# Loading every weight slot of a two-layer hybrid transformer step as two half-partition transfers

## What is computed

```python
mod  = silu(cond) @ w_ada[l] + b_ada[l]            # 1024 x 6144 per layer
proj = (rms_norm(x) * (1 + sc1) + sh1) @ w_in[l]   # 1024 x 1696
# three groups of heads read proj: latent attention (w_q_up, w_kv_up),
# a depthwise convolution, and a neighbourhood attention
x = x + g1 * (concat(heads) @ w_out[l])            # 1024 x 1024
h = rms_norm(x) * (1 + sc2) + sh2
# 16 experts, each token goes to 2 of them
hid = silu(h @ w_gate[e]) * (h @ w_up[e])          # 1024 x 512 each
x = x + g2 * sum_e gate[e] * (hid @ w_down[e])     # 512 x 1024
```

## Time and profile before

| what | us |
|---|---|
| median of 3 runs | 1395.42 (1394.6 to 1402.75) |
| the profiled execution, its own time | 1398.02 |
| its span in the trace | 1395.9 |
| PE busy | 1156.3 (83% of the span) |
| DVE busy | 850.8 (61%) |
| ACT busy | 662.0 (47%) |
| POOL busy | 215.2 (15%) |
| moved by DMA | 307.29 MB, of which 276.58 MB in SP's queue (q1) |

### The profile page before, as it was taken

The page is one execution under the profiler, slowest core; times in us unless marked ns, Lnnn a source line. Parts: engine busy times, 40 slices in busy tenths (PEclk is TensorE's granted clock), DMA queues, the critical chain, the costliest instruction groups (busy, mean ns, idle before and its releaser), DMA issues.

```text
span 1395.9 us, 15646 instructions
## 1 busy us (share of the span) xinstructions
PE 1156.3 (83%) x6086; PEld 947.8 (68%) x6086; DVE 850.8 (61%) x1039; ACT 662.0 (47%) x896; POOL 215.2 (15%) x187
## 2 busy tenths in 40 slices
PE   2999989998498999999829997889749899899980
PEld 1787666787477777777618776678737677777760
DVE  0147177513477888888641858832448788788853
ACT  1222444312276777787622133430237677677751
POOL 5002011000302211222003021100031122112200
PEclk9899989898699999999959996779769999999995
DMA  8865666311268899898733220002048898889833
GB/s 323 291 252 212 271 240 258 137 53 68 82 258 324 341 356 358 338 347 341 294 146 104 81 101 25 8 1 91 31 156 305 328 353 345 292 340 361 337 116 141
DMA packets 53179, 307.29 MB, mean 220 GB/s; under 512 B 11968, under 2 KB 12128, under 8 KB 19696
## 3 DMA queue, kind: packets, MB, share of 16 engines
q1 hardware_dynamic: 38304, 276.58, 52.3%
q0 software_dynamic: 13168, 23.39, 4.9%
q10 hardware_dynamic: 1632, 6.29, 1.2%
HBM read 305.00 MB, written 22.24 MB: 234 GB/s over the span
## 4 chain that ended last, share of the span: by engine, by line
PE 43%; DMA 23%; issue 15%; DVE 12%; POOL 4%; ACT 2%; POOLq 0%; DVEq 0%; ACTq 0%
DMA hg<-h_rows,h_at 19%; PE bank L926 19%; PE bank L669 9%; PE bank L658 3%; PE bank L918 3%; DVE conv_acc L1652 3%; POOL y_rows L619 2%; PE bank L786 2%; DMA ring<-wring_dram 1%; PE bank L680 1%; PE bank L713 1%; ACT y L1233 1%; PE bank L890 1%; DMA vecs<-vec_dram 1%; PE bank L772 1%
## 5 line engine op out<-in xcount | busy, mean ns | idle before, releaser
L1788 DVE TENSOR_TENSOR w_lo<-ring,w_hi 128x2048 fp32r<-128x2048 f32 x192 | 438.6, 2292 | 98.7 <-ACT w_hi L1203 98.3
L1203 ACT CAST w_hi<-ring 128x2048 fp32r<-128x2048 f32 x192 | 367.0, 1917 | 36.7 <-PE bank L926 36.7
L926 PE MATMUL bank<-w_hi,hgT_hi 128*128 128x512 f32 x512 | 203.8, 398 | 5.1 <-issue 3.2
L926 PE MATMUL bank<-w_lo,hgT_hi 128*128 128x512 f32 x512 | 201.2, 393 | 0.0
L926 PE MATMUL bank<-w_hi,hgT_lo 128*128 128x512 f32 x512 | 201.1, 393 | 0.0
L669 PE MATMUL bank<-ring,hT 128*128 128x256 f32 (+1 forms) x672 | 139.6, 368 | 2.1 <-DVE hT L1332 2.1
L669 PEld LDWEIGHTS bank<-ring,hT 128*128 128x128 f32 x672 | 122.0, 190 | 18.3 <-DVE hT L1332 2.6
L526 POOL TENSOR_TENSOR rstd<-ms,half 128x3 f32<-128x3 f32 (+3 forms) x14 | 39.8, 2842 | 516.2 <-DVE ms L1314 516.2
L619 POOL DMA_INDIRECT y_rows<-y,y_at x32 | 36.7, 1147 | 531.1 <-ACT y L1233 493.3
L926 PE MATMUL bank<-w_hi,hidT_hi 128*128 128x512 f32 x256 | 107.0, 418 | 9.9 <-DVE hidT_lo L1810 9.9
L926 PEld LDWEIGHTS bank<-w_hi,hgT_hi 128*128 128x128 f32 x512 | 97.1, 190 | 26.6 <-issue 7.0
(11 more groups left out here) (224 smaller groups left out, 1565.1 us busy)
## 6 DMA issues: line engine op xcount, KB each, us to landing
ring<-wring_dram SPq DMA_DIRECT2D x260, 1024.0 KB, 7.0
parts<-y_rows ACTq DMA_DIRECT2D x6, 1024.0 KB, 7.1
ring<-wring_dram SPq DMA_DIRECT2D x6, 640.0 KB, 4.3
h_rows<-h_tok POOLq DMA_DIRECT2D x2, 1536.0 KB, 5.9
bias<-na_bias_dram POOLq DMA_DIRECT2D x32, 64.0 KB, 5.5
x<-x_in_dram POOLq DMA_DIRECT2D x1, 1536.0 KB, 11.3
y_sample_dram<-x POOLq DMA_DIRECT2D x1, 1024.0 KB, 4.4
hg<-h_rows,h_at POOLq DMA_INDIRECT x32, 9.9
```

The source lines that it names most:

```text
L926: mm = pe.matmul(b[:, :], a, w[m], start=(start and k == 0), stop=(stop and k == 2))
L1203: act.copy(w_hi[:, q, :], in_ring(l, expert_slot(e, i))).then_inc(hi_made[q], 1)
L1788: dve.tensor_tensor(w_lo[:, q, :], in_ring(l, expert_slot(e, i)), w_hi[:, q, :], ALU.subtract) \
```

## The change

Each load of a slot becomes two, one for partitions 0 to 63 and one for 64 to 127, both in SP's queue, one right behind the other, both adding 16 to the same semaphore. All that wait for the slot wait for 32 instead of 16 per turn of the slot. Rows keep their 8 KB; SP issues 532 transfers of 512 KB (320 KB for the narrow ones) in place of 266.

```diff
         def once_loaded(l, s):
 
-            return slot_full[slot_turn(l, s)[0]], 16 * (slot_turn(l, s)[1] + 1)
+            return slot_full[slot_turn(l, s)[0]], 2 * 16 * (slot_turn(l, s)[1] + 1)
...
                     m, s = RING_ORDER[q]
                     cols = NARROW if s == S_IN + IN_LATENT or S_UP <= s < S_OUT else SLOT
-                    sp.dma_start(ring[:, q % RING, 0:cols], wring[m * LAYER_SLOTS + s, :, 0:cols]) \
-                      .then_inc(slot_full[q % RING], 16)
+                    for ps in (slice(0, P // 2), slice(P // 2, P)):
+                        sp.dma_start(ring[ps, q % RING, 0:cols], wring[m * LAYER_SLOTS + s, ps, 0:cols]) \
+                          .then_inc(slot_full[q % RING], 16)
                     q += 1
```

## The result

The changed kernel took 1711.0 us (median of 4 runs, 1700.8 to 1711.5) against 1399.1 for the kernel before: a ratio of 1.222, 95% interval 1.216 to 1.228. It is slower, as forecast, but by 312 us and not by 128, and lies outside the stated range of 1396 to 1700. The profiled execution took 1700.8, its span 1698.6.

What follows compares the result with a forecast made beforehand. It took the experts' 19.5 us lap of scatter, gather, transposes and down products as the bound. Laps 103, first slices 10, start and bursts 15 made 128 us on 1395.4: 1523 us, range 1396 to 1700.

Steps and rivals of the forecast that it cites:

- What bounds the kernel now: Experts: a lap of 19.5 us of scatter, gather, transposes and down products sets the pace; its longest piece is the gather.
- SP's issues, semaphore packets, waits: Ring loads: 266 more issues of 0.33 us, hidden; sixteen more small packets per slot, nothing; PE and ACT wait for later half.
- The speed of a half: Ring loads to 64 partitions: a byte costs 1.5 times one to all partitions, with ends of 1.0 and 2.0.
- The basis of that step: Engine shares of `bias` transfers to 64 partitions: 61.1 engine-us per MB against 42.1 or 38.2, so 1.45 to 1.60 times.
- The sum: Whole kernel at 1.5: experts' laps 19.5 to 23.8 us, 103 in all, plus 10 and 15, is 128 us more.
- the first slices: First slices of both groups of experts: 324 GB/s x 1.5 exceeds 423, costing 5 us each, 10 in all.
- Start and bursts: Before layer 0's experts: eight slots needed at the start cost 10 us, a burst of four at 146 us costs 5.
- lock step: Rival, ring loads: all 16 engines write one half at once, factor 2, laps of 31.4 us, 1783 us; chance 0.22.
- The argument against lock step: Experts: gather and scatter give more rows to some engines than to others, so engines drift apart.
- The estimate by 328/196 = 1.67: Ring loads, by the skill page's rates for 128 and 64 partitions: a lap of 26.4 us and about 1610 us.
- Signs in the profile: Expected trace: DMA share 9 tenths, landings some 15 us, gathers 12 to 14, SP's waits shorter or gone, more ring waits.
- The risk named last: PE, waiting more, loses clock (0.91 with pauses against 1.00 without), adding a few us to each layer.

Runs made afterwards that it cites:

- (7): Kernel before, with each gather issued one turn earlier on POOL, ahead of the scatter it stood behind: 1338.4 us, ratio 0.957.
- (3): Against the kernel before, each slot loaded as two halves of the columns, each to all 128 partitions: 1383.9 us, ratio 0.989.
- (1): Transfers alone, kernel's work left out, 20 loads per shape: whole slots 422 GB/s, partition halves in turn 218, lower half alone 206, 32 to 95 422.
- (6): Against the kernel before, partition halves only for the 74 slots outside the experts, whole loads for the experts: 1428.5 us, ratio 1.022.
- (8): Changed kernel with each gather issued one turn earlier: 1707.7 us, ratio to the kernel before 1.222, against 1711.0 without it.

## Why the prediction was wrong

Point by point, by its own steps:

- **What bounds the kernel now**: right, and shown (7): the lap of scatter, gather, transposes and down products.
- **SP's issues, semaphore packets, waits**: each put at nothing. Right: column halves have all three and cost nothing (3). SP's issues were longer than the 0.33 us of the earlier trace rows (0.47 us at least, 0.60 in the median in the changed kernel), which its waits still hide.
- **The speed of a half**: this step failed. It read: "I take 1.5, between the two ratios and nearer to the one of lone transfers, because two neighbouring halves in one queue can overlap a little". Measured 1.90 in the steady experts, and 422 / 218 = 1.94 for the shape by itself. The upper end of 2.0 was nearly the right one, but by luck: its source, the landings of `bias` and `nav`, can't tell a rate. In the same trace a load of 24 KB lands no sooner than those of 64 and 128 KB:

```profile
y_at<-tables POOLq DMA_DIRECT2D x2, 24.0 KB, 2.3
```

- **The basis of that step**, the shares of `bias`, gave a number that is too low for a full queue. Those are lone transfers with a single 4 KB packet for each engine, so that two engines that want the same way in are often not there at the same moment; this is argued, not shown. That a full queue pays nearly the whole factor is shown (1). Of the overlap that the step counted on, little showed: two halves in turn ran at 218 GB/s where the lower half alone ran at 206 (1).
- **The sum**: its form was right. The 1.90 is worked out from the changed kernel itself, so it is no test of the form; the 1.94 of experiment 1 is. With it the sum says (29.56 x 1.94 + 2.1) / 423 = 140.5 us for 90, a lap of 30.4, and 30.1 was measured. 24 laps at 10.6 us more are 254 of the 278.5 us that the two groups of experts took more, where 103 had been forecast. The other 24 stand against the 10 for the first slices. Start and bursts were put at 15 us and cost 25 in the whole change and 33 alone (6). Most of it is the start: the first matmuls of the projection came at 66.9 us in place of 47.6, 19.3 later, where 10 had been counted. Layer 1's projections and heads: nothing, and -1.3 measured.
- **The rival lock step** was the true case by its price, at a chance of 0.22. It gave 1783 us for 1711. Its lap of 31.4 was 1.3 too long, some 30 us in 24 laps, since the factor is 1.90 and not 2. The rest, some 40 us, comes from its 54 us for the experts' first slices and 48 for the front, which are too high. That all engines are in one half at once was not read from a trace of each engine; it is what the rates say.
- **The argument against lock step**, that gathers give more rows to some engines and so drive them apart, was wrong in its effect: with 10 gathers in 300 us the rate stayed at 229.
- **The estimate by 328/196 = 1.67**, worked out from the Trainium skill's "SBUF — State Buffer", section "Door 1: The DMA port swizzle", gave 1610 us, also too low. Those are figures for transfers of 1 MiB. The same table has an asymptote of 218 GB/s for 64 partitions, and that was the one to use for a full queue; measured 206 to 218 (1).
- **Signs in the profile.** A DMA share at 9 tenths, waits of ACT on the ring (360.3 us in 145) in place of the idle 10.4: right. Landings of some 15 us: 22.6 for a half from 490 to 790 us. Packets of q1 at 1.5 times 42 engine-us per MB: 0.945 x 16 x 300 / 64.66 = 70.2, or 1.67 times. Gathers of 12 to 14 us: 17.4. Waits on the ring in place of some of those on the gather: wrong, PE's weight loads waited 91.9 us for gathers before and 315.7 after, without this being the bound (8). SP's waits "shorter or gone": wrong, and wrong in its logic. They grew from 654.0 us to 779.8 in the whole run, in 186 waits both times. SP waits for a free slot in either regime, since a ring of six is always full of either loaded or queued slots. That wait can't tell which of the two bounds. The risk named last, that PE loses clock, came true, and cost the experts nothing that could be measured (8).

## What to carry to other kernels

A load that is cut in two should be cut along the columns, so that every piece still spans all 128 partitions; cut at partition 64, a full queue runs at half its rate (218 against 422 GB/s). When a trace has only lone, small transfers of a shape, neither their share of the engines nor their landing gives their cost in a full queue (1.45 to 1.60 and a lucky 2.0 here, for 1.94): a kernel of transfers alone, 20 of each shape, gives it in one run, and until then the range has to reach the full factor. And where an indirect transfer that stands behind another on POOL's queue is part of the longest lap, it is worth moving ahead: one turn earlier was worth 4.3% here, and nothing in the kernel that the ring bounds. A large wait is not yet a bound: PE's largest wait in the changed kernel could be removed without any gain.

## What the runs showed of the hardware that I had not expected

- 64 partitions are not slow as such: in a full queue 32 to 95 run at 422 GB/s, 0 to 63 at 206 and 0 to 31 at 204.
- Halves keep the half rate: 217 with four short loads ahead of them, 242 when SP and ACT issue one half each.
- Full-rate and half-rate pieces in one queue don't average: 260 by itself and 240 (other data included) in the kernel, where 283 was worked out.
- Smaller pieces of a bulk stream let an indirect transfer beside it land sooner: 9.9, 9.4 and 8.5 us with rows of 8, 4 and 2 KB, while the stream by itself lost 4% (422 to 406 GB/s) from 8 to 4 KB.
